# Cached key pages multiplied at the end of a job and summed before the output rows, on one Trainium2 core

## The reference

```python
def _diff_attend(q1, q2, k1, k2, v, qpos, kpos, lam):   # four heads, two score maps each
    a = probs(q1, k1) - lam * probs(q2, k2)
    return einsum('bhqk,bkhe->bqhe', a, v)

def _fox_attend(q, k, v, cq, ck, qpos, kpos):           # eight heads
    s = einsum('bqhd,bkhd->bhqk', q, k) * scale
    bias = transpose(cq)[..., :, None] - transpose(ck)[..., None, :]
    p = softmax(where(mask, s + bias, min))
    return einsum('bhqk,bkhe->bqhe', p, v)

# prompt: causal over 1024 positions, in 128-query blocks
# samples: keys and values are the 8 cached pages of each, plus the new token
ka_all = concatenate([gather(cache_diff_k), kas], axis=1)
va_all = concatenate([gather(cache_diff_v), vas], axis=1)
lf_all = concatenate([gather(cache_fox_logf), logfs], axis=1); cf_all = cumsum(lf_all, axis=1)
oa_s = _diff_attend(q1s, q2s, ...); of_s = _fox_attend(qfs, ...)
```

## Time and profile before

| | us |
|---|---|
| three runs | 1508.95, 1514.24, 1514.98 |
| median | 1514.24 |
| the profiled execution | 1509.19 |
| its span, first to last instruction | 1507.4 |

### The profile page before, as it was taken

How to read it: one execution, slowest core, us unless ns; L and a number is a source line. 1 busy time by engine, 2 the same in 40 slices (tenths; PEclk the granted TensorE clock), 3 DMA queues, 4 the chain that set the end, 5 groups by cost and what they waited for, 6 DMA issues and landing times. The chain is left out here.

```text
span 1507.4 us, 26822 instructions
## 1 busy us (share of the span) xinstructions
PE 1431.7 (95%) x10396; PEld 1290.3 (86%) x10396; DVE 855.6 (57%) x1378; ACT 637.0 (42%) x1194; POOL 365.6 (24%) x548
## 2 busy tenths in 40 slices
PE   7999989999989889879999999999999999999998
PEld 6999776777767667558789999999999999999998
DVE  6412567566554445544547876666777645444663
ACT  6723655444354434543323533323333324443543
POOL 5213876764645352021100000000000000000120
PEclk9999999999999999999999999999999999999999
DMA  5213556677755644622223222222222236655773
GB/s 183 57 34 90 178 164 210 201 231 221 237 187 178 191 158 127 220 86 71 79 82 100 70 75 69 85 85 85 75 81 78 63 140 202 201 186 185 235 259 111
DMA packets 174842, 209.93 MB, mean 139 GB/s; under 512 B 22052, under 2 KB 118892, under 8 KB 174677
## 3 DMA queue, kind: packets, MB, share of 16 engines
q1 hardware_dynamic: 174714, 208.21, 43.4%
HBM read 178.37 MB, written 29.88 MB: 138 GB/s over the span
## 5 line engine op out<-in xcount | busy, mean ns | idle before, releaser
L600 POOL TENSOR_TENSOR k_page<-k_page,q_bc 128x256 f32<-128x256 f32 x256 | 187.2, 763 | 132.2 <-DMA k_page<-in_cache_fox_k 100.3
L1197 PE MATMUL PS<-ht_hi,w_hi 128*128 128x344 f32 x576 | 195.9, 340 | 5.9 <-ACT z_raw L724 2.5
L1197 PE MATMUL PS<-ht_hi,w_lo 128*128 128x344 f32 x576 | 186.4, 324 | 0.0
L1197 PE MATMUL PS<-ht_lo,w_hi 128*128 128x344 f32 x576 | 186.3, 323 | 0.0
L2415 PE MATMUL PS<-act_hi,wd_hi 128*128 128x344 f32 x528 | 169.0, 320 | 2.6 <-DVE act_lo L2253 2.6
L2415 PE MATMUL PS<-act_hi,wd_lo 128*128 128x344 f32 x528 | 168.6, 319 | 0.0
L2415 PE MATMUL PS<-act_lo,wd_hi 128*128 128x344 f32 x528 | 168.4, 319 | 0.0
L2250 DVE TENSOR_TENSOR wd_lo<-wd_raw,wd_hi 128x1024 fp32r<-128x1024 f32 (+1 forms) x88 | 87.8, 1002 | 115.6 <-ACT act_hi L2064 95.5
L832 ACT ACTIVATE probs<-probs,stat 128x256 f32<-128x256 f32 (+7 forms) x128 | 98.8, 773 | 127.3 <-DVE stat L1076 126.7
L1197 PEld LDWEIGHTS PS<-ht_hi,w_hi 128*128 128x128 f32 x576 | 110.4, 192 | 31.6 <-issue 23.9
L2061 ACT ACTIVATE wd_hi<-wd_raw 128x1024 fp32r<-128x1024 f32 (+1 forms) x88 | 74.2, 845 | 140.8 <-DMA act_raw<-a_dram 104.9
(11 more groups left out here) (280 smaller groups left out, 3283.9 us busy)
## 6 DMA issues: line engine op xcount, KB each, us to landing
wd_raw<-in_w_down SPq DMA_DIRECT2D x44, 512.0 KB, 3.5
...
```

Source lines behind the costliest of these rows:

```text
L600: ins = pool.tensor_tensor(kpage[:, g % 2, c:c + PIECE], kpage[:, g % 2, c:c + PIECE], qbc[:, c:c + PIECE], ALU.mult)
L1197: ins = pe.matmul(PS[0:rows, z_bank(c), 0:THIRD], b[:, k, :], a[:, k, third(i)], start=(k == 0 and p == 0), stop=(k == KC - 1 and p == 2))
```

## The change

Nothing is computed otherwise; work is placed otherwise.

- The page list starts at job 1 instead of 0, so each key page has the next place in it, and value pages of all samples but the last come a job later.
- POOL multiplies the pages of a job at the end of its job, behind `rope` and `head_stat`, instead of right behind `split_lo`.
- DVE sums the pages of J-1 right behind `weights(J-1)`, ahead of `rows_out(J-2)` (diff) and of the copies for the samples' softmax, instead of behind them. `head_norm` is one job later.
- PE's fb step goes from the middle to the end of a job, ahead of the transposes of J-1.
- In the last unit PE makes the scores of J behind the transposes of J-2's second map instead of at the job's start, and DVE takes the first maximum behind the copies of those transposes.
- Transposes of normed rows for `merge` (`turn_jobs`) go from jobs 57, 59, 61, 62 to 59, 61, 64, 65.
- POOL's `mix` goes from the end of `project` to the start of `merge`.

```diff
--- before.py
+++ after.py
@@ -284,7 +284,8 @@
 
     TILES = [("q", u) for u in range(MAPS)] + [(kind, u) for u in range(MAPS) for kind in "kv"]
     norm_job = lambda v: 4 * NT + 3 + 5 * v // 2
-    turn_jobs = {NJ - 7: (0, 0), NJ - 5: (1, 0), NJ - 3: (0, 1), NJ - 2: (1, 1)}
+    turn_jobs = {NJ - 5: (0, 0), NJ - 3: (1, 0), NJ: (0, 1), NJ + 1: (1, 1)}
+    LAST_UNIT = NJ - NT
     FT = 4
     FIRST = [(0, 0), (1, 0), (0, 1), (0, 2), (1, 1), (1, 2)]
     chunk_of = lambda n, i: FIRST.index((n, i)) if n < 2 else 3 * n + i + (3 if n >= FT else 0)
@@ -315,15 +316,15 @@
         u, t = unit(J), tile(J)
         return {0: [("v", u, 0)], 1: [("v", u, 1)], 2: [("s", u)], 3: [("k", u, 0)], 4: [("k", u, 1)]}.get(t, [])
 
-    k_slots = [J for J in range(NJ) for _ in range(1 + (tile(J) == 5))]
-    k_job = lambda g: k_slots[g - EARLY_PAGES] if g >= EARLY_PAGES else -1
+    k_slots = [J for J in range(1, NJ) for _ in range(1 + (tile(J) == 5))]
+    k_job = lambda g: k_slots[g - EARLY_PAGES] if g >= EARLY_PAGES else 0
 
     def v_job(g):
 
         b, n = divmod(g, PAGES)
         if b == DB - 1:
             return ready(b) + 5 + n // 2
-        first = 8 + 7 * b
+        first = 9 + 7 * b
         twice = [J for J in range(first, first + 7) if tile(J) in (5, 6)][-1]
         return sorted(list(range(first, first + 7)) + [twice])[n]
 
@@ -335,8 +336,8 @@
 
     def soft_at(J):
 
-        return ([("fb", b) for b in at_job(J, 1)] + [("mt", b) for b in at_job(J, 2)] + [("nm", b) for b in at_job(J, 3)]
-                + [("ls",)] * (J == LS) + [("ml",)] * (J == ML))
+        return ([("mt", b) for b in at_job(J, 2)] + [("nm", b) for b in at_job(J, 3)]
+                + [("ls",)] * (J == LS) + [("ml",)] * (J == ML) + [("fb", b) for b in at_job(J, 1)])
 
     blocks_of = lambda t: [(c, min(4, t + 1 - c)) for c in range(0, t + 1, 4)]
     turns_of = lambda J, m: [("t", J, m, c, nblk) for c, nblk in blocks_of(tile(J))]
@@ -395,6 +396,34 @@
     kv_out = lambda kind, u: ((io["o_dk"], io["o_dv"]) if u < 4 else (io["o_fk"], io["o_fv"]))[kind == "v"]
     kv_sample = lambda kind, u: ((io["o_sdk"], io["o_sdv"]) if u < 4 else (io["o_sfk"], io["o_sfv"]))[kind == "v"]
     columns = lambda u: slice(u % 4 * P, (u % 4 + 1) * P)
+
+    def sample_mix(pool):
+
+        def mix(out, a, b, op):
+            pool.tensor_tensor(out, a, b, op).then_inc(mix_step, 1)
+
...
+    io["sample_mix"] = sample_mix
 
     with nc.Block() as block:
 
@@ -524,7 +553,7 @@
                 if n < len(TILES):
                     load_w(n)
                 for g in range(EARLY_PAGES, DB * PAGES):
-                    if max(0, k_job(g - 2) + 1) == J:
+                    if k_job(g - 2) + 1 == J:
                         load_key_page(g)
                 if u == MAPS - 1 and t == 1:
                     sp.wait_ge(chunk_done, NC)
@@ -647,10 +676,6 @@
                 n = {1: k_tile(u + 1) + 1, 5: k_tile(u + 2)}.get(t, len(TILES))
                 if n < len(TILES):
                     split_lo(n)
-                for g in k_pages(J):
-                    if g % PAGES == PAGES - 1:
-                        later_pages(g // PAGES)
-                    multiply(g)
                 if J:
                     for c, h in fill(J - 1)[0] + fill(J - 1)[1]:
                         if h:
@@ -662,32 +687,13 @@
                 for v in range(NT):
                     if norm_job(v) + 1 == J:
                         head_stat(v)
-
...
             pool.wait_ge(zn_in, 80)
             pool.tensor_tensor(qk_new[0:DB], z_new[0:DB, 0:2, :], z_new[0:DB, 2:4, :], ALU.mult).then_inc(qk_done, 1)
...
 
         @block.scalar
         def _(act):
@@ -1101,14 +1107,18 @@
             for J in range(NJ + 3):
                 if J >= 3 and fox(J - 3):
                     rows_out(J - 3)
-                if J < NJ:
+                if J < LAST_UNIT:
                     maximum(J, 0)
                 if 2 <= J < NJ + 2 and fox(J - 2):
                     turned(J - 2)
+                if LAST_UNIT <= J < NJ:
+                    maximum(J, 0)
                 if J < NJ:
                     maximum(J, 1)
                 if 1 <= J <= NJ:
                     weights(J - 1)
+                for g in range(2, EARLY_PAGES) if J == 0 else k_pages(J - 1):
+                    reduce_page(g)
                 if 2 <= J < NJ + 2 and not fox(J - 2):
                     rows_out(J - 2)
                 if J < NJ:
@@ -1132,12 +1142,10 @@
                             dve.tensor_copy(l_all[0:DB, :], bank_of(e)[0:DB, 2 * MAPS:4 * MAPS]).then_inc(dve_evac, 1)
                 for b in at_job(J, 5):
                     sums(b)
-                for g in range(2, EARLY_PAGES) if J == 0 else k_pages(J - 1):
-                    reduce_page(g)
                 for b in at_job(J, 1):
                     page_maxima(b)
                 for v in range(NT):
-                    if norm_job(v) + 2 == J:
+                    if norm_job(v) + 3 == J:
                         head_norm(v)
                 if J in turn_jobs:
                     turned_lo(*turn_jobs[J])
@@ -1388,13 +1396,15 @@
 
             for J in range(NJ + 3):
                 before, after = fill(J) if J < NJ else ([], [])
-                if J < NJ:
+                if J < LAST_UNIT:
                     scores_of(J)
                 if J >= 3 and fox(J - 3):
                     wait_evacuated(pe, ("o", J - 3))
                     pe.transpose(bank(("b", J - 3))[:, 0:P], ot[:, (J - 3) % 2, :], ident[:, :]).then_inc(x_done, 1)
                 if 2 <= J < NJ + 2 and fox(J - 2):
                     turn(J - 2, 1)
+                if LAST_UNIT <= J < NJ:
+                    scores_of(J)
                 if J in turn_jobs:
                     turn_attention(*turn_jobs[J])
                 for c, half in before:
@@ -1406,11 +1416,14 @@
                     weighted_sum(J - 2)
                 if J < NJ:
                     for e in soft_at(J):
-                        soft(e)
+                        if e[0] != "fb":
+                            soft(e)
                     for g in v_pages(J):
                         value_page(g)
                 for c, half in after:
                     chunk(c, (half,))
+                for b in at_job(J, 1):
+                    soft(("fb", b))
                 if 1 <= J <= NJ:
                     turn(J - 1, 0)
 
@@ -1586,6 +1599,7 @@
                 pool.wait_ge(pool_step, n_step)
                 pool.tensor_tensor(out, ms, expo, ALU.pow).then_inc(done, 1)
 
+            io["sample_mix"](pool)
             pool.memset(gap, 0.0).then_inc(zeroed, 1)
             pool.memset(st[:, 3, :], -0.5).then_inc(zeroed, 1)
             pool.wait_ge(zeroed, 3)
```

46 lines of the change are left out of this document (24 added, 22 removed).

## The result

| | us |
|---|---|
| changed kernel, median of 6 runs | 1530.93 (1524.62 to 1536.52) |
| kernel before, 6 runs beside it | 1514.61 (1508.95 to 1519.12) |
| ratio, 95% interval | 1.0097 (1.007 to 1.0124) |
| profiled execution after, and its span | 1531.28, 1529.2 |

The change makes the kernel about 16 us slower. The forecast was no difference; the time lies above its range of 1499 to 1527.

What follows compares the result with a forecast made beforehand. PE, busy 95% of the span, was taken as the bound. Units 0 to 6 +2.8, last unit -2.2, block end -1.3 made -0.7 us; taking the median of 1514.24 gave 1513.5, stated as 1514, range 1499 to 1527.

Steps and rivals of the forecast that it cites:

- POOL is late because of its own order alone: Jobs of tile 5: POOL makes a weight tile's low parts before multiplying two pages, so DVE waits, 2.50 us in job 22.
- The stalls of the sums ahead of the rows: Jobs 6, 14, 22, 30: PE idles 3.9 to 5.2 us each before the transposes, awaiting DVE's output rows; 18.1 us lost.
- my 15.2: Units 0 to 6, sums ahead of rows: 18.1 us of stalls, less 7.4 for joined maps, plus 4.5 for tile-7 rows.
- The 4.5 us for the rows of tile-7 jobs: Jobs of tile 7: PE waits 1.1 us for output rows in each of four units; bounds 0 and 8.
- The clock: Three drops of PE's clock beside the four new stalls, 1.6 us each: +4.7 (bounds 0 and 6.4); other drops counted gone.
- The fb step: PE's samples' step, moved to the end of a job, finds its bank and gate sums ready: 4.3 us gained.
- The last unit: Weighted sums' waits of 7.1 us go, 3.5 and 1.4 come back through ACT's copies: -2.2 us (bounds -5 and +2).
- rival (c): Last unit: the wait moves from weighted sums to transposes one for one; 1516 to 1518; within the forecast's chance of 0.50.
- the gains of the shifted list at jobs 40 and 46 to 48: Shorter stalls and fewer clock drops: 2.5 us gained at job 40, 4.6 at jobs 47 and 48.
- my 17.1: All gains in units 0 to 6: rotary steps 2.5, fb step 4.3, clock drops 3.2, job 48 4.6, job 40 2.5 us.
- the barrier: End of the block: with POOL's combination moved to the next block, the barrier waits for DVE instead of POOL: -1.3 us.
- Rival (b): Slower: POOL's product, three steps later in tiles 1 to 3, sets the pace in more jobs; 1526, chance 0.22.

Runs made afterwards that it cites:

- a1: The changed kernel with DVE summing the pages again behind the output rows and softmax copies, all else as changed: 1507.67 us, 0.9946 of the kernel before.
- b2: The kernel before with one part of the change alone, DVE summing the pages ahead of the output rows and softmax copies: 1539.30 us, ratio 1.016.

## Why the product is late

**Pages ahead of the low parts on POOL in jobs of tile 5**, in the changed kernel (a5) and in the kernel before (b1):

```diff
+                if t == 5:
+                    pages(J)
                 if n < len(TILES):
                     split_lo(n)
...
+                if t != 5:
+                    pages(J)
```

(`pages(J)` holds the loop over `k_pages(J)`.)

> The changed kernel, but in jobs of tile 5 POOL multiplies the two pages ahead of the low parts of the weight tile, which it otherwise waits 4 to 5 us for; DVE still sums the pages ahead of the output rows. Undoing the order of the sums brought 23 us back, so what makes them late is asked here. Theory P (the product is late because the low parts stand in front of the pages): the four stalls in jobs 6, 14, 22 and 30 and the joined maps' waits go while the order of the sums stays; some stalls of a bare 1.6 us (the sum and the rows) remain: 1530.9 - 18 = 1513 (bounds 1509 and 1518). Rival T (the pages' own transfers, or DVE's 2.4 us of sums by themselves, hold the rows): 1525 or above.

> The kernel before with that one edit: pages ahead of the low parts in jobs of tile 5. Theory P: the 7.4 us of waits for the joined maps in jobs of tile 7 go, no new wait takes their place: 1514.9 - 7 = 1508 (bounds 1506 and 1511). Rival: the second page's transfer (0.92 us late in job 21) or the output rows of the job take their place one for one: 1513 to 1516.

Measured: a5 1533.78 us, 1.0123 (1.0104 to 1.0143); b1 1509.77, 0.9968 (0.9948 to 0.9988). The step "POOL is late because of its own order alone" falls: a5 gains nothing, and its four stalls are 4.0, 3.6, 2.7 and 5.5 us. b1 is 6 us faster by its median, but not as expected: the waits for the joined maps are 7.4 us as before, and where its gain lies is open. Its timelines in jobs 21 to 23, POOL, DVE, SP (whose columns are the same, the instruction being the issue of a transfer) and PE:

```profile
320.68 2.80 POOL L600 TENSOR_TENSOR k_page<-k_page,q_bc 128x256 f32<-128x256 f32 x4 [5.48 <-DMA k_page<-in_cache_fox_k]
...
311.73 1.21 DVE L1006 TENSOR_REDUCE scores<-k_page 128x16 f32<-128x1024 f32 x1
...
323.51 1.22 DVE L1006 TENSOR_REDUCE scores<-k_page 128x16 f32<-128x1024 f32 x1 [3.52 <-POOL k_page L600]
...
313.57 0.33 SPq L472 DMA_DIRECT2D v_page<-in_cache_diff_v  x1
314.00 0.38 SPq L472 DMA_DIRECT2D v_page<-in_cache_fox_v  x1
...
315.66 0.33 SPq L462 DMA_DIRECT2D k_page<-in_cache_diff_k  x1
316.10 0.38 SPq L462 DMA_DIRECT2D k_page<-in_cache_fox_k  x1
...
328.83 0.98 PE L1321 MATMUL PS<-ident,probs 128*128 128x128 f32 x7 [3.34 <-DVE probs L1058]
```

The buffer is free at 312.9, when the sum of the page before it in that buffer ends. SP issues the load only at 315.66, behind a value page, and POOL starts at 320.68. With two buffers, sum, load and product are a round: the load waits for the sum of the page before it in its buffer, the product for the load, and the next sum for the product.

**The pairs moved to tile 3**, in the changed kernel (e2) and in the version d1, below (e3):

```diff
-    k_slots = [J for J in range(1, NJ) for _ in range(1 + (tile(J) == 5))]
+    k_slots = [J for J in range(1, NJ) for _ in range(1 + (tile(J) == 3))]
```

> The changed kernel (1530.9 us) with the jobs that take two pages moved from tile 5 to tile 3; the sums stay ahead of the rows. Theory D (two sums of 1.2 us and the wait for the second page, 0.9 us, meet DVE's heaviest job, that of tile 6; with one page there the rows come 2 us sooner): PE's stalls of 2.8 to 5.3 us in jobs 6, 14, 22 and 30 fall to 1 to 2 us each and two or three clock drops go: 1530.9 - 8 - 4 = 1519 (bounds 1515 and 1523). Rival (any sum ahead of the rows holds PE there, or the stall moves to jobs of tile 4): 1527 to 1533.

> The version with the sums behind the rows, sample 6's value pages in jobs 51 to 56 and the last unit's order undone (1498.4 us), with the two-page jobs moved from tile 5 to tile 3. Theory D: the waits for the joined maps in jobs of tile 7 (5 us) and a clock drop or two go: 1493 (bounds 1490 and 1496). Rival (the buffers' round of sum, load, product is the pace, wherever two pages stand): 1497 to 1502.

Measured: e2 1541.74 us, 1.0173 (1.0151 to 1.0196); e3 1511.27, 0.9971 (0.9953 to 0.9988): 11 and 13 us slower than the same with the pairs in tile 5. Theory D falls. In e2 the stalls moved with the pairs, as its rival said: jobs 14, 22 and 30 have none over 0.8 us, jobs 12, 20 and 28 have 6.1, 4.2 and 4.8 us. Job 12, POOL, DVE and PE (POOL waits here for the next sample's query):

```profile
253.36 2.76 POOL L629 TENSOR_TENSOR k_page<-k_page,q_bc 128x256 f32<-128x256 f32 x4 [5.24 <-DMA q_bc<-qs_dram]
...
256.16 1.22 DVE L1006 TENSOR_REDUCE scores<-k_page 128x16 f32<-128x1024 f32 x1 [5.15 <-POOL k_page L629]
...
257.78 1.09 PE L1323 MATMUL PS<-ident,probs 128*128 128x128 f32 x4 [6.10 <-DVE sample_gate_sums L1130]
```

**SP issues key pages ahead of value pages**, in d1 (g1), and with POOL's pages first as well (g2):

```diff
+                for g in range(EARLY_PAGES, DB * PAGES):
+                    if k_job(g - 2) + 1 == J:
+                        load_key_page(g)
                 for g in range(DB * PAGES):
                     if (v_job(g - 2) if g >= 2 else v_job(0) - 2) == J:
                         load_value_page(g)
```

(and the loop of key pages gone from its old place)

> The version with the sums behind the rows, sample 6's value pages in jobs 51 to 56 and the last unit's order undone (1498.4 us), with one edit: in each job SP issues the key pages' loads ahead of the value pages' loads. Theory Q (the key page stands in SP's queue behind value pages; but POOL still multiplies it behind the low parts): the waits for the joined maps (5.2 us in all) fall by a third, value pages come no later than needed: 1496 (bounds 1494 and 1499). Rival (the sum that a key page's load waits for comes late in the job, and the value pages, now behind it, come late for PE): PE waits for value pages rise above 4 us, 1502 or more.

> The same edit, and in jobs of tile 5 POOL multiplies the pages ahead of the low parts. Theory Q+P (the late product has two causes, each of which hides the other's removal: SP's order and POOL's order): DVE waits under 1 us for the second product of the pairs, the waits for the joined maps fall under 1.5 us: 1498.4 - 4 - 1.7 = 1493 (bounds 1490 and 1495). Rival: as for the first edit alone, 1502 or more, or no change beyond it.

Measured: g1 1516.21 us, 1.0007 (0.999 to 1.0024); g2 1508.78, 0.9955 (0.993 to 0.998). Both are slower than d1's 1498.39. The rival holds: PE waits 19.5 and 22.2 us for value pages, which now stand behind SP's waits for sums.

The waits for the joined maps do go: none stands among g1's waits, 1.7 us in g2, 5.2 in d1. But that does not show that the product came in time, since PE itself came later, held by value pages (2.1 us in job 14, 2.6 in job 23). What shows it is DVE's own wait for the second product of the pair:

| us | job 6 | job 14 | job 22 | job 30 |
|---|---|---|---|---|
| before | 1.02 | 1.52 | 2.50 | 1.52 |
| b1, POOL's pages first | 1.03 | 2.68 | 3.52 | 1.50 |
| d1 | 0.94 | 1.51 | 1.52 | 2.26 |
| g1, SP's key pages first | 0.94 | 1.51 | 1.52 | 0.32 |
| g2, both | 0.27 | 1.17 | 0.61 | 0 |

Job 22 in d1, g1 and g2:

```profile
314.74 1.22 DVE L1008 TENSOR_REDUCE scores<-k_page 128x16 f32<-128x1024 f32 x1 [1.52 <-POOL k_page L631]
...
317.96 1.22 DVE L1008 TENSOR_REDUCE scores<-k_page 128x16 f32<-128x1024 f32 x1 [1.52 <-POOL k_page L631]
...
319.43 1.22 DVE L1014 TENSOR_REDUCE scores<-k_page 128x16 f32<-128x1024 f32 x1 [0.61 <-POOL k_page L631]
```

Either order changed by itself leaves most of these waits as they were or makes them longer; both together shorten all four. That is what theory Q+P says: the late product has two causes, SP's order and POOL's, and each hides the other's removal. (PE came late in g1 as well as in g2, so its lateness does not explain the difference between them.) That it also gains time is not shown, since the value pages took more than it could give. g2's median is 7 us under g1's; in the profiles PE is busy 1431.3 us in g2 and 1436.8 in g1, so most of that is clock.

## The value pages behind a 2 MB load

In the changed kernel SP issues in jobs 57 and 58, and PE waits in job 59:

```profile
624.48 0.43 SPq L560 DMA_DIRECT2D wo_raw<-in_w_o  x1
624.96 0.50 SPq L525 DMA_DIRECT2D out_o_fv<-v_rows  x1
625.50 4.48 SPq L537 DMA_DIRECT2D od_dram<-o_part  x1
630.73 1.44 SPq L501 DMA_DIRECT2D v_page<-in_cache_diff_v  x1
632.26 0.44 SPq L501 DMA_DIRECT2D v_page<-in_cache_fox_v  x1
...
638.23 1.03 PE L1381 MATMUL PS<-v_page,scores 128*4 128x256 f32 x8 [3.79 <-DMA v_page<-in_cache_fox_v]
...
640.41 1.03 PE L1381 MATMUL PS<-v_page,scores 128*4 128x256 f32 x8 [1.15 <-DMA v_page<-in_cache_fox_v]
```

The first line is the 2 MB load, the third the store of sample 6's sums. Before, that store was issued in job 57, in 0.33 us and ahead of the 2 MB load. The list of value pages, one job later, puts it in job 58, behind that load.

**The load a job earlier** (a3), and **sample 6's value pages in jobs 51 to 56**, in the changed kernel (e4) and in a1 (c1):

```diff
-                if u == MAPS - 1 and t == 1:
+                if u == MAPS - 1 and t == 0:
                     sp.wait_ge(chunk_done, NC)
```

```diff
+        if b == DB - 2:
+            return (51, 52, 53, 53, 54, 54, 55, 56)[n]
         first = 9 + 7 * b
```

> The changed kernel with the first load of the output projection's weights (2 MB) issued in job 56 instead of 57, and nothing else. In the changed kernel the shift of the value pages puts this load right ahead of the store of sample 6's sums and of the value pages of jobs 58 to 60; the store took 4.48 us to issue, PE waited 3.79 and 1.15 us for value pages, and the clock fell. Theory V (the load in front of the small transfers is the cause): the 6.5 us of PE's waits for value pages fall under 2 and one clock drop goes: 1530.9 - 4.5 - 2 = 1524.5 (bounds 1523 and 1527). Rival: the value pages are late because they and their store themselves stand a job later: no change, 1529 to 1532.

> The changed kernel (1530.9 us) with sample 6's value pages in jobs 51 to 56, and nothing else. Theory V (value pages behind the 2 MB load cost the changed kernel 6.5 us of waits and the clock behind them): 1530.9 - 9 = 1522 (bounds 1520 and 1525). Rival (with PE already 15 us late at the last unit, the transfers have time and only the order of the last unit holds PE): 1527 to 1531.

> The changed kernel with the sums back behind the rows (1507.7 us) and the eight value pages of sample 6 in jobs 51 to 56 instead of 51 to 57, two pages in jobs 53 and 54, so that the store of its sums is issued in job 57 ahead of the 2 MB weight load, and job 57 has no value page, as before. Theory V (in the last unit the shifted value list costs PE 8.3 us of waits for value pages and a clock drop): waits for value pages under 2 us, 1507.7 - 8 = 1499.5 (bounds 1497 and 1503). Rival: the last unit's own order makes the transfers late, and the loss stays: 1506 to 1509.

Measured: a3 1528.99 us, 1.0105 (1.0055 to 1.0155), too wide to tell. In its profile the store is issued in 1.41 us instead of 4.48, but value pages still end 5.1 us of waits instead of 6.5. e4: 1525.21, 1.0068 (1.0048 to 1.0087): 5.7 us less than the changed kernel by the medians, though the intervals just overlap. c1: 1498.21, 0.9904 (0.9878 to 0.9931): 9.5 us less than a1. PE's waits for value pages are 1.0 us in c1, 8.3 in a1. Theory V holds for the list, at 60% of its size in the changed kernel and in full in a1: sample 6's value pages a job later cost 6 to 9 us. That the 2 MB load is what makes them late is not shown: a3 took the load out of the way and most of the waits stayed.

## The last unit, and the rest

**The last unit's order undone**, in the changed kernel (a4) and in c1 (d1): `LAST_UNIT = NJ` instead of `NJ - NT`.

> The changed kernel with one part undone: in the last unit the scores and the first maximum stand again at the start of the job; all else as changed. From job 55 to the first product of the output projection the changed kernel loses 12.0 us against before, of which 7.4 are the value pages. Theory O (scores behind the transposes delay the exponentials, and ACT's copies of the sums come late): 3 of the other 4.6 us come back although the waits of the weighted sums (6 us) return: 1528. Rival W (the order in the last unit gains what I forecast, 2.2 us, and the loss is only clock and value pages): the time rises to 1533.

> The version with the sums behind the rows and sample 6's value pages in jobs 51 to 56 (1498.2 us), with one more part undone: in the last unit the scores and the first maximum stand again at the start of the job. Theory of the forecast (the order in the last unit gains 2.2 us): 1500.4. Rival O (it loses: from job 54 to the first product of the output projection this version gives back 3.2 of the 14.0 us that it was ahead of the kernel before, with nothing left there but this order): 1495 to 1496.

Measured: a4 1530.53 us, 1.0092 (1.0065 to 1.0119); d1 1498.39, 0.988 (0.9861 to 0.99): no difference from the kernel each starts from. In the profiles, from job 55 to `merge` c1 loses 3.0 us against before (-13.8 to -10.8), d1 0.9 (-17.0 to -16.1). The waits say why: with the new order the weighted sums' fall from 6.6 to 1.1 us in both pairs, and those for ACT's copies, in front of `o_transposed` and the transposes, rise from 8.3 to 14.7 us (a4 to the changed kernel) and from 8.9 to 15.4 (d1 to c1). So neither theory has the number: the wait moves and grows by 1 us, the order gives nothing, and by the profiles it costs at most 2 us.

**The lists alone on the kernel before** (e1):

```diff
-    k_slots = [J for J in range(NJ) for _ in range(1 + (tile(J) == 5))]
-    k_job = lambda g: k_slots[g - EARLY_PAGES] if g >= EARLY_PAGES else -1
+    k_slots = [J for J in range(1, NJ) for _ in range(1 + (tile(J) == 5))]
+    k_job = lambda g: k_slots[g - EARLY_PAGES] if g >= EARLY_PAGES else 0
...
-        first = 8 + 7 * b
+        if b == DB - 2:
+            return (51, 52, 53, 53, 54, 54, 55, 56)[n]
+        first = 9 + 7 * b
```

> The kernel before with the page lists shifted by one job and sample 6's value pages in jobs 51 to 56, and nothing else of the change. The version with all of the change but the order of the sums is 17 us faster than before. Theory G (the shifted lists make most of it, since the first page of each sample gets its query a job earlier against the maxima, and the stalls of jobs 40 and 48 go): 1515 - 10 = 1505 (bounds 1502 and 1508). Rival (the gains come from the other parts: rope first, fb at the end, the combination in the next block, which cost 0 to 2.7 us each when undone): 1510 to 1514.

Measured: 1504.30 us, 0.9932 (0.9908 to 0.9956): 12 us faster than before. Theory G holds: the lists make most of the gain.

**POOL's combination back** in the attention block (d3) and **POOL's products back** ahead of the rotary steps (d4), each in c1:

> The same version (1498.2 us) with POOL's combination of the samples' parts back at the end of the attention block. Theory of the forecast (the barrier then waits for POOL instead of DVE, 2.1 us against 0.8, and the combination costs nothing in the next block): 1499.5. Rival (the combination holds DVE's and PE's work at the start of the next block by as much or more): 1496 to 1498.

> The same version (1498.2 us) with POOL's products again right behind the low parts, ahead of the rotary steps. Theory of the forecast (PE's projection pieces wait 2.5 us again for ACT and POOL, at the end of job 3): 1500.7. Rival (the product, then three POOL steps earlier in tiles 1 to 3, lets the next page be loaded earlier, since a page's buffer is loaded again only when it is summed, and so shortens the waits for the joined maps and the rows, 12 us in all in this version): 1495 to 1497.

Measured: d3 1506.26 us, 0.9922 (0.9897 to 0.9947); PE waits 2.7 us at the barrier instead of 0.8. d4 1502.11, 0.9906 (0.9886 to 0.9926); PE's pieces wait 1.2 us for ACT. Both medians lie above c1's, on the side of the forecast, and by more than its 1.3 and 2.5 us; the intervals of the ratios both overlap c1's. Neither is settled.

The best versions are c1 and d1: all of the change but the order of the sums (d1 also without the last unit's order), with sample 6's value pages closer together. They take 1498 us, 1.0 to 1.2% less than before and 32 us less than the changed kernel.

## Why the prediction was wrong

**The stalls of the sums ahead of the rows: right in place, and nearly in size.** The four in jobs 6, 14, 22 and 30 measure 3.3, 3.4, 2.8 and 5.3 us, 14.8 in all for 18.1. The joined maps' waits shrank from 7.4 to 2.3 us, and b2 shows 14.3 us net for my 15.2. The 4.5 us for the rows of tile-7 jobs did not come: only job 7 has a wait over 0.8 us, and a1 has it too.

**The reason I gave for them was wrong in part.** I put the late second product down to POOL's low parts. With these out of the way POOL waits for the transfer (b1), and only SP's order and POOL's together shorten DVE's waits (g2). And DVE waited only 0, 0.86, 0.86 and 3.31 us for the product, 5.0 of the 14.8: for the most part DVE's two sums of 1.2 us behind the joined maps made the stalls. That the size came out so near is in part luck.

**The clock: the step that failed most.** I took three drops at 1.6 us for the four long stalls, +4.7 (three times 1.6 is 4.8), and three and a half drops gone elsewhere, -5.6: about -1 in all. PE was busy 13.6 us longer after. By the stretches that is 11.9 us beside the stalls of jobs 5, 6, 7, 14, 22 and 30, less 10.2 for the four of before, which all went, plus 11.9 that the sum put at nothing: 5.1 beside the gate sums' waits in jobs 47 and 54, 5.1 beside the value pages', 1.7 near the end. Over all executions the clock's part is about 8 us, still 9 above the forecast. Two readings were at fault. The earlier trace rows had shown 2.59 us without a drop, and I read from it that only the long stalls count; the rows after show the clock at 0.68 and 0.74 by stalls of 1.45 and 2.01 us. And I took the price of a drop from 4 us of one that lasted 8. The low stretches also lie under long products: at 396 us PE was busy for all four us at 0.50, nearly all of it with scores of job 31.

**The fb step: its gain was counted, its debt not.** The 4.3 us went to 0 as said. But the transposes now directly behind it need its copy, and DVE's sums stand ahead of that copy too: 6.2 us of new waits in the changed kernel, 0.6 in a1.

**The value pages: missing from the sum.** I named SP's queue for the query only. The shift moved a store and a job's value pages behind the 2 MB load: 5.7 us in the changed kernel by the medians of e4.

**The last unit: wrong sign or nothing.** The weighted sums' waits went from 7.1 to 1.1 us as said. I put 4.9 us (3.5 and 1.4) against that for ACT's copies; with the order alone changed these waits grew by 6.4 us (a4 to the changed kernel), so the wait came back whole, as rival (c) had it.

**Right:** the gains of the shifted list at jobs 40 and 46 to 48 (21.4 to 8.1 us in the table; e1 gives 12 us alone), somewhat less than my 17.1 for all gains up to there; the barrier (2.12 to 0.81 us, PE 0.48 us behind DVE's last instruction); the combination at no cost to PE. Rival (b) had the sign and, with 1526, nearly the time, but not the mechanism: between jobs 8 and 14 the table shows no loss, and tiles 1 to 3 are there.

The terms put right: -0.7, plus 3.4 for the order of the sums with its clock (23.3 for 19.9), 3.4 for gains that were less (13.7 at job 50 in a1 for 17.1), 5.7 for the value pages, 2.2 to 4.2 for the last unit: 14.0 to 16.0 us, for 16.3 measured. The clock is spread over these terms and not one of them. The reckoning is made after the fact and takes the 13.7 us from single profiles, of which that of before was 5 us under its median; that it meets the measured time so closely is in part luck.
